# Running sums read back as DRAM rows, and block sums on VectorE, in a 2-layer decoder trunk (one core)

## What is computed

```python
def layernorm(x, g, b):
    mu = jnp.mean(xf, axis=-1, keepdims=True)
    var = jnp.mean(jnp.square(xf - mu), axis=-1, keepdims=True)
    y = (xf - mu) * lax.rsqrt(var + LN_EPS) * g + b
def ssd_chunked(xdt, a_dt, bm, cm, init_state):       # chunks of 128 tokens, 16 heads in 4 groups
    a_cs = jnp.cumsum(ac, axis=-1)                     # running sum of the decays
    decay_in = jnp.exp(segsum(ac))                     # exp(a_cs[l] - a_cs[s]) for s <= l, else 0
    cb = jnp.einsum('bclgn,bcsgn->bcgls', cc, bc)
    y_diag = jnp.einsum('bcgls,bgrcls,bcsgrp->bclgrp', cb, decay_in, xc)
    ...
    y_off = jnp.einsum('bclgn,bcgrpn,bgrcl->bclgrp', cc, prev_states, jnp.exp(a_cs))
def chunk_gmlp(u, v, ln_g, ln_b, w_s, b_s):
    u = jax.nn.gelu(u)
    v = layernorm(jax.nn.gelu(v), ln_g, ln_b)
    ...                                                # a 128x128 mix of v over tokens, per group
    return u * mixed, v
```

## Time and profile before

| | us |
|---|---|
| median of 3 runs (1393.98, 1396.18, 1398.44) | 1396.18 |
| the profiled execution | 1395.54 |
| its span, first to last instruction | 1393.8 |
| TensorE busy in it | 1342.9 (96%) |
| VectorE busy | 370.7 (27%) |
| ScalarE busy | 178.1 (13%) |
| mean granted TensorE clock | 0.986 of full speed |

### The profile page before, as it was taken

The page is one execution under the profiler, slowest core; times in us unless marked ns, Lnnn a source line. Parts: engine busy times, 40 slices in busy tenths (PEclk is TensorE's granted clock), DMA queues, the critical chain, the costliest instruction groups (busy, mean ns, idle before and its releaser), DMA issues.

```text
span 1393.8 us, 18198 instructions
## 1 busy us (share of the span) xinstructions
PE 1342.9 (96%) x7707; PEld 860.1 (62%) x7707; DVE 370.7 (27%) x825; ACT 178.1 (13%) x376; POOL 62.0 (4%) x87
## 2 busy tenths in 40 slices
PE   6999998999999999989999999999999999999986
PEld 5888887888888888758755534434343443444432
DVE  3535885321111016933300010201111011011112
ACT  1231324010001001042100000000000100100002
POOL 2003310000000102000000000000000000000000
PEclk9999999999999999999999999999999999999998
DMA  8536722564546333410999999999999999999994
GB/s 265 205 124 237 263 91 91 182 202 128 176 149 211 99 121 121 128 43 16 352 402 402 402 397 398 392 402 394 405 399 393 403 392 404 387 377 404 390 404 196
DMA packets 169666, 381.48 MB, mean 274 GB/s; under 512 B 7660, under 2 KB 63516, under 8 KB 169530
## 3 DMA queue, kind: packets, MB, share of 16 engines
q1 hardware_dynamic: 161571, 358.96, 69.5%
q0 software_dynamic: 3184, 11.40, 2.7%
q10 hardware_dynamic: 4834, 9.99, 2.2%
HBM read 372.41 MB, written 9.01 MB: 274 GB/s over the span
## 4 chain that ended last, share of the span: by engine, by line
PE 88%; DVE 6%; DMA 3%; SPq 1%; issue 1%; ACT 1%; ACTq 0%; DVEq 0%
PE ps L1711 30%; PE ps L2176 16%; PE ps L2241 13%; PE ps L2191 8%; PE ps L2201 4%; DVE region L1415 3%; PE ps L1937 3%; PE ps L2252 2%; DMA big<-in_moe_w_down_dram 1%; PE ps L2133 1%; PE ps L2095 1%; PE ps L2144 1%; PE ps L2218 1%; DMA big<-in_w_in_even_dram 1%; PE ps L1720 1%
## 5 line engine op out<-in xcount | busy, mean ns | idle before, releaser
L1711 PE MATMUL ps<-big 128*128 128x264 f32 x1376 | 314.9, 391 | 3.4 <-DMA big<-in_w_in_even_dram 3.4
L1711 PEld LDWEIGHTS ps<-big 128*128 128x128 f32 x1376 | 264.3, 193 | 50.2 <-DMA big<-in_w_in_even_dram 3.5
L2176 PE MATMUL ps<-big,region 128*64 128x384 f32 (+3 forms) x1200 | 217.7, 459 | 6.5 <-DMA big<-in_moe_w_gate_dram 3.5
L2176 PEld LDWEIGHTS ps<-big,region 128*64 128x64 f32 (+1 forms) x1200 | 115.5, 147 | 104.3 <-issue 62.1
L1711 PE MATMUL ps<-region,big 128*128 128x264 f32 x704 | 160.0, 390 | 3.7 <-ACT region L965 3.7
L2241 PE MATMUL ps<-big,region 128*64 128x512 f32 (+1 forms) x608 | 157.6, 609 | 2.2 <-DMA big<-in_moe_w_down_dram 1.6
L1711 PEld LDWEIGHTS ps<-region,big 128*128 128x128 f32 x704 | 134.4, 192 | 27.3 <-issue 4.1
L2191 PE MATMUL ps<-big,region 128*64 128x384 f32 (+1 forms) x720 | 111.0, 460 | 0.0
L2241 PEld LDWEIGHTS ps<-big,region 128*64 128x64 f32 (+1 forms) x608 | 50.5, 146 | 95.0 <-issue 91.3
L2191 PEld LDWEIGHTS ps<-big,region 128*64 128x64 f32 x720 | 51.3, 137 | 56.6 <-issue 49.0
L1626 DVE TENSOR_TENSOR region<-region,ps 128x384 f32<-128x384 f32 (+1 forms) x24 | 12.1, 520 | 225.5 <-PE ps L2176 225.5
(11 more groups left out here) (371 smaller groups left out, 1032.0 us busy)
## 6 DMA issues: line engine op xcount, KB each, us to landing
big<-in_moe_w_up_dram SPq DMA_DIRECT2D x48, 1536.0 KB
big<-in_moe_w_gate_dram SPq DMA_DIRECT2D x40, 1536.0 KB
big<-in_moe_w_down_dram SPq DMA_DIRECT2D x40, 1536.0 KB
big<-in_w_in_even_dram SPq DMA_DIRECT2D x10, 2048.0 KB
big<-in_moe_w_gate_dram SPq DMA_DIRECT2D x16, 1024.0 KB
big<-in_moe_w_up_dram SPq DMA_DIRECT2D x16, 1024.0 KB
big<-in_moe_w_down_dram SPq DMA_DIRECT2D x16, 1024.0 KB
region<-in_moe_w_gate_dram SPq DMA_DIRECT2D x8, 1536.0 KB
```

Of the source, the lines that this page charges most:

```text
L1711: ins = mm(ps[:, 0:T], w[:, c, cols:cols + P], src[:, c, :], start=c == 0, stop=c == nk - 1)
L2176: ins = mm(out, xg[:, 4 * j + c, 0:cap], w[:, c, r, :], start=j + c == 0, stop=j + c == 4)
```

## The change

First, `cr` goes. TensorE computes the running sums once more in `cs`, as rows (32 rows of 128, one for each head and chunk). ScalarE copies them to SBUF (`cst`) and writes them to a DRAM buffer `csd`; four broadcast DMAs on ScalarE's queue bring eight rows each back onto all 128 partitions (`CR`, two buffers in the place of `GV`). VectorE's subtraction and ScalarE's exponential read `CR` instead of PSUM. Second, the eight matmuls of each of the two statistics of v become one: VectorE first adds up the eight blocks, seven additions that each wait for the one before, and `stat_one` multiplies the sum by the ones. Several semaphores are also renamed.

```diff
-    add("cs", ("cs_ready", 1))
+    add("cs", ("cs_ready", 1), ("dt_act", 4))
...
-            add(("cr", i), *((("seg_ready", 4 * i + 4),) + ((("ecs_ready", i - 3),) if i >= 4 else ())))
...
+        csd = nc.dram_tensor("cs_rows", [32, P], F32).ap()
+        cst = big[32:64, 25600:25600 + P]
+        CR = [reg(8496 + 1024 * n, 1024).rearrange("p (k m) -> p k m", k=2) for n in range(2)]
...
+            act.wait_ge(sem("cs_ready"), 1)
+            a.activation(cst, tile("cs")[0:32, 64:192], ACT.Copy).then_inc(sem("dt_act"), 1)
+            act.wait_ge(sem("dt_act"), 4)
+            act.dma_start(csd, cst).then_inc(sem("x_loaded"), 16)
             act.wait_ge(sem("tot_ready"), 2)
...
+            def broadcast_cs(j):
+
+                act.dma_start(CR[j % 2].rearrange("p k m -> p (k m)"),
+                              csd[8 * j:8 * j + 8, :].rearrange("(a h) l -> a (h l)", a=1).broadcast_to([P, 1024])).then_inc(
+                    sem(f"rows_in{j % 2}"), 16)
+
+            act.wait_ge(sem("x_loaded"), 80)
+            act.wait_ge(sem("gout_ready"), 1)
+            broadcast_cs(0)
+            broadcast_cs(1)
...
+                if k in (1, 3):
+                    broadcast_cs(2 + k // 2)
                 if k >= 4:
                     if k >= 6:
                         act.wait_ge(sem("cs_scaled"), k - 5)
-                    a.activation(ecs[:, k % 2], tile(("cr", k))[:, :].rearrange("p (r l) -> p r l", r=4),
+                    act.wait_ge(sem(f"rows_in{k // 2 % 2}"), 48)
+                    a.activation(ecs[:, k % 2], CR[k // 2 % 2][:, k % 2].rearrange("p (r l) -> p r l", r=4),
                                  ACT.Exp).then_inc(sem("ecs_ready"), 1)
...
+                if k == 2:
+                    dve.wait_ge(sem("gv_ready"), 2)
+                    then(v.tensor_tensor(rstd[:, :], GV[:, 0, :], GV[:, 1, :], ALU.add))
+                    for c in range(2, DC):
+                        dve.wait_ge(sem("gv_ready"), c + 1)
+                        ins = v.tensor_tensor(rstd[:, :], rstd[:, :], GV[:, c, :], ALU.add)
+                        if c < DC - 1:
+                            then(ins)
+                        else:
+                            ins.then_inc(sem("sq_summed"), 1)
                 if k == 3:
                     layer_norm_mean("lnv_mean", GV, "gv_cent")
+                    for c in range(1, DC):
+                        dve.wait_ge(sem("vsq_ready"), c + 1)
+                        ins = v.tensor_tensor(SQ1[:, 0, :], SQ1[:, 0, :], SQ1[:, c, :], ALU.add)
+                        if c < DC - 1:
+                            then(ins)
+                        else:
+                            ins.then_inc(sem("sq_summed"), 1)
...
-                    filled(dve, ("cr", k))
+                    dve.wait_ge(sem(f"rows_in{k // 2 % 2}"), 16 * (k // 4 + 2))
...
+                    filled(dve, ("cb", k))
                     dve.wait_ge(sem("dec_ready"), k + 1)
...
+            def stat_one(name, at, total):
+
+                pe.wait_ge(sem("stat_read"), STATS.index(name))
+                pe.wait_ge(sem("sq_summed"), at)
+                mm(STAT[:, 0:T], ones[:, :], total, start=True, stop=True).then_inc(sem("stat_full"), 1)
...
-                        for c in range(DC):
-                            stat("lnv_mean", "gv_ready", 0, GV, c)
+                        stat_one("lnv_mean", 1, rstd[:, :])
                     if s == 1 and j == 0:
-                        for c in range(DC):
-                            stat("lnv_var", "vsq_ready", 0, SQ1, c)
+                        stat_one("lnv_var", 2, SQ1[:, 0, :])
...
-            done(mm(ps[:, 32:64], ones[:, :], adt[:, 0:32], start=True, stop=True))
+            mm(ps[:, 32:64], ones[:, :], adt[:, 0:32], start=True, stop=True)
+            done(mm(ps[0:32, 64:192], adt[:, 0:32], upper[:, :], start=True, stop=True))
...
-                    ps = claim(("cr", k))
-                    for r in range(4):
-                        h = 16 * q + 4 * g + r
-                        ins = mm(ps[:, P * r:P * (r + 1)], adt[:, h:h + 1].broadcast_to([P, P]), upper[:, :],
-                                 start=True, stop=True)
-                    done(ins)
```

More of the change, by code:

```diff
@@ L488, in _ @@
             sp.dma_start(prow[0:120, 3, :], dw[128:248]).then_inc(sem("par_loaded"), 16)
-            sp.dma_start(wsn, i["gmlp_w_s"][0].rearrange("g i j -> i g j")).then_inc(sem("ws_loaded"), 16)
-            sp.dma_start(cbrows, i["state_ssd_conv"][0].rearrange("b k n -> (b k) n")).then_inc(sem("cb_loaded"), 16)
+            sp.dma_start(wsn, i["gmlp_w_s"][0].rearrange("g i j -> i g j")).then_inc(sem("rows_in0"), 16)
+            sp.dma_start(cbrows, i["state_ssd_conv"][0].rearrange("b k n -> (b k) n")).then_inc(sem("rows_in1"), 16)
             sp.dma_start(row16[0:1, 0:8], i["gmlp_w_s"][0, :, 0, 0:1].rearrange("g a -> a g"),
@@ L654, in _ @@
                    allow_small_or_imprecise_dtypes=True).then_inc(sem("const_ready"), 1)
-            pool.wait_ge(sem("ws_loaded"), 16)
+            pool.wait_ge(sem("rows_in0"), 16)
             g.affine_select(out=wsn, in_=wsn, compare_op=ALU.is_ge, fill=0.0, base=0,
@@ L734, in fetch_rows @@
                     out=xrow[0:cap, :], out_offset=None, in_=hrows[:, :],
-                    in_offset=bass.IndirectOffsetOnAxis(ap=rowidx[0:cap, 0:1], axis=0)).then_inc(sem("rows_loaded"), 16)
+                    in_offset=bass.IndirectOffsetOnAxis(ap=rowidx[0:cap, 0:1], axis=0)).then_inc(sem("rorows_in0"), 16)
             pool.wait_ge(sem("crw_stored"), 32)
@@ L1299, in _ @@
                         h = 4 * g + r
-                        v.scalar_tensor_tensor(out=dec[:, k % 2, r], in0=tile(("cr", k))[:, P * r:P * (r + 1)],
+                        v.scalar_tensor_tensor(out=dec[:, k % 2, r], in0=CR[k // 2 % 2][:, k % 2, P * r:P * (r + 1)],
                                                scalar=ncs[:, 16 * q + h:16 * q + h + 1], in1=negm[:, :],
                                                op0=ALU.add, op1=ALU.add).then_inc(sem("seg_ready"), 1)
+                    filled(dve, ("cb", k))
                     dve.wait_ge(sem("dec_ready"), k + 1)
@@ L1578, in rows_known @@
                 if s:
-                    dve.wait_ge(sem("rows_loaded"), t * 16 + 16 * s)
+                    dve.wait_ge(sem("rorows_in0"), t * 16 + 16 * s)
                 v.tensor_copy(rowidx[0:cap, :], psum[4][0:cap, BLK * P:BLK * P + 1]).then_inc(sem("rows_known"), 1)
@@ L1761, in _ @@
                 done(ins)
-            pe.wait_ge(sem("cb_loaded"), 16)
+            pe.wait_ge(sem("rows_in1"), 16)
             ps = claim("cbufT")
@@ L2088, in turn_rows_in @@
             def turn_rows_in(cap, value, n4, n5):
-                pe.wait_ge(sem("rows_loaded"), value)
+                pe.wait_ge(sem("rorows_in0"), value)
                 for half, n in enumerate((n4, n5)):
```

2 lines of the change are left out of this document (1 added, 1 removed).

## The result

The changed kernel takes 1407.72 us (median of 6 runs, 1403.17 to 1409.61) where the kernel before takes 1394.15 in the same session (6 runs, 1393.46 to 1398.44): 1.0088 times as long, 95% interval 1.0072 to 1.0105, that is 12.3 us more by the ratio; the medians lie 13.6 us apart. Forecast were 5.9 us more, 1402 and a range up to 1406: the sign is right, the size half of what came, and the time lies above the range. The profiled execution took 1408.35 us with a span of 1406.4.

The account below looks back on a forecast made before the run. VectorE paces the loop and TensorE, busy 96%, follows. Mixes 5.6 us late, minus 2.2 in the loop, plus 2.5 of half clock: 5.9 us on 1396.18, so 1402; range 1397.5 to 1406.

Parts of the forecast that it names:

- a stall at the first statistic: TensorE waits for VectorE's first sum, idle some 6.9 us; u goes on 3.6 us later than before.
- mixes late through ScalarE's queue: Row copy, DMA issue and table load on ScalarE put the mixes at 176.3 instead of 170.78, 5.6 us late.
- the half clock behind it: Behind the last y of the loop TensorE's clock falls to half through fst and output projection, costing 2.5 us.
- the rival without this fall: Clock does not fall at the end of the loop: +3.4 us, 1399.6; chance 0.22.
- the path to the loop: From the statistics over VectorE and ScalarE to the mixes: 5.6 us late, first subtraction at 186.6 instead of 181.03.
- costs little: A clock fall after the first stall is likely but absorbed by TensorE's wait for the second sum, 2.9 us slack.
- the same collision in sample 3: GpSimd's scaling, 1.93 us, gets in VectorE's way once in sample 3, which runs 141.7 to about 148.
- The gain of 2.2 at k=1: In the loop, VectorE's one wait for TensorE, 2.17 us ahead of k=1, falls away.
- I take no change: Loop subtractions reading SBUF instead of PSUM take the same time; other bound 1.6 us less or as much more.
- just in time: TensorE's z of k=1 ends about 189.9, when the exponential needs it; lateness there bounded at 0.5 us.
- The rival of a further fall ahead of the mixes: Clock falls there too, z of k=1 comes 1.5 to 2.5 us late, VectorE waits: +8 us, 1404; chance 0.15.
- The rival "faster": TensorE's 13.1 us are really saved, given early sums and shorter loop steps: about 1390 or 1383; chance 0.07.

Follow-up runs that it names:

- e2: Changed kernel with only VectorE's sums for the two statistics; cr back on TensorE, no DRAM rows: ratio 1.0055 to the kernel before, 1402.06 us.
- e12: Changed kernel with GpSimd's scaling of sample 4 held back until the first sum is done: ratio 1.0059 to the kernel before, 1402.00 us.
- e5: Changed kernel with nineteen unused 128x264 matmuls ahead of the first statistic, filling TensorE's stall: ratio 1.0080 to the kernel before, 1405.94 us.
- e1: Changed kernel with only the DRAM rows; both statistics of v again eight matmuls each: ratio 1.0030 to the kernel before, 1400.10 us.
- e3: Changed kernel with GpSimd's last scaling held until the subtractions of k=2 are done: ratio 1.0059 to the kernel before, 1403.99 us.
- e13: Changed kernel with the first sum made behind sample 1 instead of sample 2: ratio 1.0078 to the kernel before, 1406.15 us.
- e10: Kernel before plus DMA rows with earlier cs, sample instructions spread over the loop, GpSimd's last scaling held, old statistics: ratio 0.9958, 1389.36 us.

## Why the prediction was half right

**Right.** TensorE's busy share was no measure of the gain; the distance grew by 10.0 us although 13.1 us of matmuls were taken out. The order of the losses held: a stall at the first statistic, a short one at the second, mixes late through ScalarE's queue, a gap of 5 us ahead of the last y (forecast 4.9) and the half clock behind it (2.0 and 2.5 in two executions, forecast 2.5). For the rival without this fall the prediction had the gap of 2.96 us that did nothing; e2 shows a gap of 2.95 with a fall, so that row bore less than it seemed. The broadcasts were covered. The additions cost 0.47 each (e12: 2.77 for six).

**First mis-sized term: the path to the loop, +5.6 forecast, +7.0 measured** (first subtraction 188.08 - 181.03; 0.3 us of it is the second u, which ended that much later). The sentence that failed is that a fall of the clock after the first stall "costs little", with 2.9 us of slack. It put the second sum's wait for ScalarE's squares at nothing; this was 1.56 us. The slack was TensorE's own, and the wrong one to look at. The fourth u came late by a stall 1.8 us longer than forecast and by the half clock (three projections of u in 12.15 us, in e5 10.84); its GELU stands on ScalarE ahead of the squares, and the second sum needs the squares. In e5, with the same late start but neither fall nor wait, the sum was ready at 156.17, in the changed kernel at 157.54.

The 1.8 us more of the stall are the additions' collision with GpSimd: they ended at 143.46, where the prediction took 141.7, with 143.7 as the upper bound. e12 shows the collision. On VectorE's own path it cost nothing against the forecast, which had priced the same collision in sample 3; sample 3 then took 5.0 us without one, and the mean began at 148.41, forecast 148.2. That this came out even is luck: two misplaced terms, one in each direction.

**Second, the loop: -2.2 forecast, +1.2 measured** (40.30 against 39.14 between first and eighth subtraction). The gain of 2.2 at k=1 came, as e1 shows. Against it stand 2.4 us at k=2, the larger miss, where the prediction said of the subtractions from SBUF "I take no change", with 1.6 us as the other bound. It had read the exclusion between VectorE and GpSimd off the subtraction of the mean and priced it once, in sample 3, but did not ask the same for an operand that moves from PSUM to SBUF. e3 shows it. And 0.8 to 0.9 us at k=1: "just in time" was too late, the exponential waited for the late z. The rival of a further fall ahead of the mixes named that mechanism; the mixes at half clock (5.44 us) are in both profiles of the changed kernel, and not in e5 and e13, where this wait is 0.77.

**The sum** is then 5.9 + 1.4 + 3.4, less 0.5 for the clock behind the loop, 10.2, against 10.27 us by which the output projection starts later. The measured 12.3 are 2 us more. In the profiled execution most of them lie at the end: the last four matmuls (eight records) run at half clock and take 5.44 us (the window at 1394), where before they took 3.6 and the clock fell behind the last of them. The second profile of the changed kernel did not have this, yet the ratio of its session is the same 1.0088; so how much of the last 2 us is fixed and how much chance stays open. A difference of 10.3 us lies within both intervals.

**The rival "faster"** was rightly rejected, but its condition was taken too narrowly. It asked for sums that are ready earlier; e13 made the first one so and gained nothing that can be told. What it said of the loop (steps below 4.8 us) is what e10 did, with the rows and with VectorE's sample work spread.

## What to carry to other kernels

Work moved off the busiest engine pays only if the receiving engine has room before the next thing that the first one needs from it; lay the two timelines side by side between two fixed places, and add up what the receiving engine must do in between. Moving the stall within that stretch gained nothing here. If two engines run a loop at nearly the same pace, each relief alone is worth little (here 0.7 us), and both together can be worth much more (8.5). And when an operand moves from PSUM to SBUF, look for GpSimd instructions in the same stretch, even where the instruction itself gets no longer.

## What the hardware showed that was not expected

The subtraction of k=2 lost more, 2.39 us, than GpSimd's scaling lasted, 1.92, and undisturbed it would have ended at 197.96, 0.3 us before that scaling is recorded to start. What is recorded on GpSimd at that moment is the issue of a DMA (197.32, 0.93 us). In e3 both the issue and the scaling are recorded at the same distance from the subtraction, and nothing is lost; there the scaling has to wait for the subtraction. This points to a claim that the scaling makes ahead of its recorded start; how far ahead, no run shows. Elsewhere a scaling recorded with 2.14 and one with 2.82 us cost VectorE 1.6 each (additions 4.36 against 2.77; sample 3 in e12, 2.81 against 1.22).

The places at which the clock falls are few and much the same in most of these kernels (near 88, 112, 620 to 636, 680, 1290 to 1300, 1370 and at the end), but which of them it takes differs from kernel to kernel, and between two executions of one. Windows of the changed kernel, first and second profile, for the earlier trace rows:

```profile
110.00:116.00 6.00, 6.00 (x17) 4.83 (x17) 0.52 (x2) 0.00 (x0) 3.81 (x2) 0.50 0.60 233
```

```profile
110.00:116.00 6.00, 6.00 (x28) 5.15 (x28) 0.52 (x2) 0.39 (x1) 3.82 (x2) 1.00 0.71 261
```

The same code, 17 matmul records in one and 28 in the other. In e10's profile the clock is at 1.00 near 620, 680, 1290 and 1370, and from the output projection to the end it takes 1150.3 us, where e1, which has the falls near 620, 680 and at the end, takes 1156.8. That is a spread of 6.5 us behind the place where these changes end, as large as the forecast effect; with it the time of a single execution can't tell a change of 0.3%. The distance between two fixed places tells more, but it too moved by 2.0 us between two executions of the changed kernel, through the length of the half clock alone but for 0.3 us.
